# Attention of a two-block transformer on one core: the reciprocals' diagonal on ScalarE, the normed output kept in PSUM, and a new order of the projections

## The reference

```python
# first block: 8 local heads, each 64 wide, on an 8 x 64 grid
scores = jnp.einsum('brqhd,brkhd->bhrqk', qg, kn) * (dh ** -0.5) + bias[None]
p = jax.nn.softmax(jnp.where(mask, scores, NEG_INF), axis=-1)
o = jnp.einsum('bhrqk,brkhd->brqhd', p, vn)
# and 12 dilated heads in 3 groups (dilation 1, 4, 16), merged by their log-denominators
# second block: 16 query heads, 4 key heads, 512 latent and 256 context tokens
def gqa_attend(q, k, v):
    s = jnp.einsum('bkgqd,bksd->bkgqs', q, k, preferred_element_type=jnp.float32) * (HEAD_DIM_2 ** -0.5)
    p = jax.nn.softmax(s, axis=-1).astype(v.dtype)
    return jnp.einsum('bkgqs,bksd->bkgqd', p, v)
```

## Time and profile before

| | us |
|---|---|
| median of 3 runs | 2993.64 |
| lowest, highest | 2989.40, 2996.92 |
| the profiled execution | 3000.23 |
| its span, first to last instruction | 2998.4 |
| mean granted TensorE clock | 0.957 of full |

### The profile page before, as it was taken

How to read it: one execution, slowest core, us unless ns; L and a number is a source line. 1 busy time by engine, 2 the same in 40 slices (tenths; PEclk the granted TensorE clock), 3 DMA queues, 4 the chain that set the end, 5 groups by cost and what they waited for, 6 DMA issues and landing times. The chain is left out here.

```text
span 2998.4 us, 37915 instructions
## 1 busy us (share of the span) xinstructions
PE 2673.7 (89%) x14592; PEld 2178.1 (73%) x14592; DVE 1583.5 (53%) x2351; ACT 1041.3 (35%) x1815; POOL 1144.4 (38%) x654
## 2 busy tenths in 40 slices
PE   1799889989999888889699999997899999699998
PEld 1576567768887666666488888885787888488886
DVE  2444536654454436556665555555567686522223
ACT  2343333332222444444421122114456555422222
POOL 2235534534444422232333333333344444344443
PEclk9899999989999899999799999998899999799999
DMA  5444214433343100000133333321111111022221
GB/s 198 150 166 148 92 61 140 137 127 134 120 140 127 36 22 19 19 19 26 43 131 114 109 126 126 113 99 51 46 51 56 43 57 57 22 92 93 97 99 70
DMA packets 80547, 267.74 MB, mean 89 GB/s; under 512 B 8560, under 2 KB 14320, under 8 KB 80368
## 3 DMA queue, kind: packets, MB, share of 16 engines
q1 hardware_dynamic: 70416, 248.67, 24.0%
q10 hardware_dynamic: 9664, 15.34, 1.6%
q0 software_dynamic: 288, 1.31, 0.1%
HBM read 260.57 MB, written 4.72 MB: 88 GB/s over the span
## 5 line engine op out<-in xcount | busy, mean ns | idle before, releaser
L1975 POOL TENSOR_TENSOR SLO<-RAW,SHI 128x1024 fp32r<-128x1024 f32 (+1 forms) x336 | 817.0, 2433 | 1309.2 <-ACT SHI L1809 1309.0
L1809 ACT ACTIVATE SHI<-RAW 128x1024 fp32r<-128x1024 f32 (+1 forms) x336 | 346.3, 1033 | 1117.5 <-PE PS L2238 1084.6
L2236 PE MATMUL PS<-HLh,SHI 128*128 128x512 f32 x1680 | 690.3, 411 | 28.2 <-DVE HLl L2044 17.6
L2237 PE MATMUL PS<-HLl,SHI 128*128 128x512 f32 x1680 | 662.6, 394 | 0.0
L2238 PE MATMUL PS<-HLh,SLO 128*128 128x512 f32 x1680 | 662.2, 394 | 0.0
L2236 PEld LDWEIGHTS PS<-HLh,SHI 128*128 128x128 f32 x1680 | 320.2, 191 | 128.2 <-issue 48.3
L2238 PEld LDWEIGHTS PS<-HLh,SLO 128*128 128x128 f32 x1680 | 319.6, 190 | 69.2
L2236 PE MATMUL PS<-hh,SHI 128*128 128x512 f32 (+1 forms) x944 | 356.4, 378 | 13.3 <-DVE hl L2128 9.9
L2237 PEld LDWEIGHTS PS<-HLl,SHI 128*128 128x128 f32 x1680 | 320.8, 191 | 65.0 <-issue 7.0
L2237 PE MATMUL PS<-hl,SHI 128*128 128x512 f32 (+1 forms) x944 | 348.6, 369 | 0.0
L2238 PE MATMUL PS<-hh,SLO 128*128 128x512 f32 (+1 forms) x944 | 348.3, 369 | 0.0
(11 more groups left out here) (233 smaller groups left out, 4015.8 us busy)
## 6 DMA issues: line engine op xcount, KB each, us to landing
RAW<-in_k_w SPq DMA_DIRECT2D x316, 512.0 KB, 3.2
ADA<-in_k_w SPq DMA_DIRECT2D x132, 512.0 KB, 4.1
early<-in_k_w SPq DMA_DIRECT2D x12, 512.0 KB, 10.0
RAW<-in_k_w SPq DMA_DIRECT2D x20, 256.0 KB, 2.6
XL<-in_xT ACTq DMA_DIRECT2D x1, 2048.0 KB, 12.5
bi<-in_k_bias ACTq DMA_DIRECT2D x16, 128.0 KB, 3.0
out<-XL SPq DMA_DIRECT2D x8, 256.0 KB, 2.1
bi<-in_k_bias ACTq DMA_DIRECT2D x8, 192.0 KB, 3.7
```

The lines of the kernel that those rows point to most:

```text
L1809: eng.activation(u.hi, u.w, ACT.Copy).then_inc(S["a_hi"], 1)
L1975: eng.tensor_tensor(u.lo, u.w, u.hi.bitcast(F32), ALU.subtract).then_inc(S["g_lo"], 1)
L2236: eng.matmul(st.out, lh, rh, start=st.first and j == 0, stop=False)
L2237: eng.matmul(st.out, lh, rl, start=False, stop=False)
```

## The change

The reciprocals' diagonal is made by ACT, as a copy of the identity with the reciprocal as scale, in place of POOL. Its place in a round moves: first reciprocals and diagonals, then the output split. `onorm` writes its product to columns 256 to 383 of the bank itself, and the split reads it from there; the bank is given back after the low half. Empty yields ahead of a rotated projection's key are four and not two. The first local pair and its values go into the dense list, and the list has another order: v 0 comes right behind k 0, v 1 behind k 1, v 2 behind the second dilated group; the turned values (a write to memory and a read in another order) move with them.

```diff
@@ attention
-            t_rec, t = tick("v_rec"), tick("g_share")
+            t_rec, t = tick("v_rec"), tick("a_share")
...
-            put(OutNorm(b.ap, o.ap, t_mm, o.free, t_rb, t))
-            give(b, t)
-            return o, t
+            put(OutNorm(b.ap, o.ap, b.ap[:, 256:384], t_mm, o.free, t_rb, t))
+            o.free = [t]
+            return b, t
...
+            if turn:
+                for it in pairs[i - 2]:
+                    shares(it)
             if read:
                 finish(pairs[i - 3][0], *done)
                 if "done" in pairs[i - 3][1]:
                     emitted.add(pairs[i - 3][1]["done"])
-            if turn:
-                for it in pairs[i - 2]:
-                    shares(it)
...
-    def out_split(o, t_o, src, hi, lo, t_free):
+    def out_split(bank, t_o, src, hi, lo, t_free):
         t1, t2 = tick("a_ohi"), tick("v_olo")
         put(OutSplit(src, hi, lo, t_o, t_free, t1, t2))
-        o.free = [t1, t2]
+        give(bank, t2)
         return [t1, t2]
@@ dl_qk, and the same in qk2
-            yield
-            yield
+            for _ in range(4):
+                yield
             emitted.add(f"dilated {which} {g} {j}")
@@ the first attention
-    run(bgz(pipelined([na_qk(0, "q"), na_qk(0, "k")])))
...
-    for j in range(1, 4):
+    for j in range(4):
         dense += [after(f"na {j - 2} scored")] if j > 1 else []
         dense += [na_qk(j, "q")]
-        dense += [dl_turned(j - 2)] if j > 1 else []
-        dense += [na_qk(j, "k"), dl_values(j - 1)]
-    dense += [dl_qk(0, 0, "q"), dl_turned(2), dl_qk(0, 0, "k")]
-    dense += [dl_qk(0, g, w) for g in (1, 2) for w in "qk"]
+        dense += [dl_turned(j - 1)] if 0 < j < 3 else []
+        dense += [na_qk(j, "k")]
+        dense += [dl_values(j)] if j < 2 else []
+    dense += [dl_qk(0, g, w) for g in range(2) for w in "qk"]
+    dense += [dl_values(2), dl_qk(0, 2, "q"), dl_turned(2), dl_qk(0, 2, "k")]
@@ ScalarE
+            def share(st):
+                a.wait_ge(st.t_rec, st.t_dfree, d_const)
+                eng.activation(st.dg, ident, ACT.Copy, scale=st.m[:, 3:4]).then_inc(S["a_share"], 1)
@@ GpSimd
-            def share(st):
-                g.wait_ge(st.t_rec, st.t_dfree, d_const)
-                eng.tensor_scalar(st.dg, ident, st.m[:, 3:4], None, ALU.mult).then_inc(S["g_share"], 1)
@@ VectorE, onorm
-                eng.tensor_tensor(st.o, st.o, st.bank[:, 0:128], ALU.mult).then_inc(S["v_onorm"], 1)
+                eng.tensor_tensor(st.out, st.bank[:, 0:128], st.o, ALU.mult).then_inc(S["v_onorm"], 1)
```

More of the change, by code:

```diff
@@ L181 @@
 Pv = namedtuple("Pv", "p nk bank values dg t_p t_v t_dg t_bank t_mm")
-OutNorm = namedtuple("OutNorm", "bank o t_mm t_free t_rb t_done")
+OutNorm = namedtuple("OutNorm", "bank o out t_mm t_free t_rb t_done")
 OutSplit = namedtuple("OutSplit", "src hi lo t_in t_free t_hi t_lo")
@@ L1002, in na_items, with na_make @@
         return res
-    def na_make(it, o, t_o):
+    def na_make(it, b, t_o):
         j, t = it["j"], it["t"]
         v = lambda a: a.rearrange("p (r c) -> p c r", r=8)[:, 16 * t:16 * t + 16, :]
-        src = o.ap.rearrange("p (c r) -> p c r", r=8)
-        oa_rdy[j] += out_split(o, t_o, src, v(oa[j][0]), v(oa[j][1]), [])
+        src = b.ap[:, 256:384].rearrange("p (c r) -> p c r", r=8)
+        oa_rdy[j] += out_split(b, t_o, src, v(oa[j][0]), v(oa[j][1]), [])
     vb = W["vb"].cells[0].ap.rearrange("p (g t n) -> p g t n", g=3, t=4)
@@ L1087, in dl_items, with dl_make @@
         return res
-    def dl_make(it, o, t_o):
+    def dl_make(it, b, t_o):
         j, r = it["j"], it["r"]
-        ob_rdy[j] += out_split(o, t_o, o.ap, ob[j][0][:, r:NT:4], ob[j][1][:, r:NT:4],
+        ob_rdy[j] += out_split(b, t_o, b.ap[:, 256:384], ob[j][0][:, r:NT:4], ob[j][1][:, r:NT:4],
                                [mtok(0, 47)] if j else [])
@@ L1140, in build_program @@
     dense += [some(bg, 32)]
-    first_out = lambda it, o, t: (na_make if "t" in it else dl_make)(it, o, t)
+    first_out = lambda it, b, t: (na_make if "t" in it else dl_make)(it, b, t)
     weave((attention(heads, W, first_out), 0.6), (bgz(pipelined(dense)), 1.0))
@@ L1358, in att_items, with make2 @@
         return res
-    def make2(it, o, t_o):
+    def make2(it, b, t_o):
         h, c0 = it["hs"], it["c0"]
@@ L1363, in make2 @@
             h.rdy = []
-        h.rdy += out_split(o, t_o, o.ap, h.hi[:, c0:c0 + 128], h.lo[:, c0:c0 + 128], h.free)
+        h.rdy += out_split(b, t_o, b.ap[:, 256:384], h.hi[:, c0:c0 + 128], h.lo[:, c0:c0 + 128], h.free)
     def out2(i, hs, stats=()):
@@ L1954, in _ @@
             own = {Dma: dma_, Table: table, Silu: silu_c, Split: split, Square: square_, Rstd: rstd_, NormA: norm_a,
-                   VCopy: vcopy, HSq: hsq, HNorm: hnorm, Score: score, Flip: flip_, OutNorm: onorm, OutSplit: osplit, Gate: gate,
+                   VCopy: vcopy, HSq: hsq, HNorm: hnorm, Score: score, Flip: flip_, Share: share, OutNorm: onorm, OutSplit: osplit, Gate: gate,
                    GSum: gsum, SiluF: silu, Up: up, LowerB: lowerb, Sigm: sigm, GateF: gate_f, GateX: gate_x,
@@ L2013, in lev_a @@
                     eng.tensor_tensor(r, r, st.q, ALU.mult).then_inc(S["g_lev"], 1)
-            own = {Dma: dma_, Split: split, Square: square_, HRope: hrope, Share: share, GateX: gate_x, DiagK: diag_k,
+            own = {Dma: dma_, Split: split, Square: square_, HRope: hrope, GateX: gate_x, DiagK: diag_k,
                    ScanQ: scan_q, LevA: lev_a}
```

## The result

The changed kernel takes 3004.47 us (median of 6 runs, 3002.88 to 3009.57) against 2992.90 for the kernel before in the same runs: ratio 1.0041, 95% interval 1.0028 to 1.0054. It is 11.6 us slower, where 12 us faster was forecast. The profiled execution has a span of 3001.9 us.

What follows compares the result with a forecast made beforehand. PE was taken as busiest but not full, with about 80 us idle in the attention stretches. First attention -17.5 and second +5.8 make about -12 us: 2981.6 against the median 2993.64; forecast alone 2973 to 2990, whole range 2966 to 3004.

Steps and rivals of the forecast that it cites:

- The diagonal's earlier time: PE's waits for dg shorten: first attention -13.4 us in local heads, -3.6 and +1.8 in dilated rounds; second -2.6 and -4.0.
- four waits in the dilated rounds: First attention: half of these waits for dg go, 2.6 us, plus 1.0 us of slow matmuls, together -3.6.
- What ScalarE adds: Second attention: diagonals at 0.40 us each make maxima up to 0.8 us later; +6 us, bounds 0 and +26.
- Output kept in PSUM: Second attention: low half no longer stretched, -2.6 us; held bank makes flips wait, +9 us, bounds 0 and +20.
- Later release: Empty yields are flushed with the tail, so waits for rotated q and k stay: 0, within 2 us.
- Rival 3: Later release does delay scores and covers part of four waits for rotated q: 9 us more, 2972; chance 0.13.
- First pair: First attention: waits at q 0 and k 0 covered, -5.7 us; flushed tails at k 2 +2.9, at d q 2 +0.5.
- The sum: First attention -17.5 us, second +5.8, net -11.7, say -12.
- rival 1: Loop through ScalarE and DVE decides, second attention +26 instead of +6: 3002 to 3009 us; chance 0.19 together with Rival 4.
- Rival 4: dg doesn't come earlier because ScalarE is late with splits: 3005 us; chance 0.19 together with rival 1.

Runs made afterwards that it cites:

- e9: Changed kernel with reciprocals and diagonals emitted behind the output split again; new order, held bank and four yields stay: ratio 0.9958 to the kernel before.
- e11: Kernel before with the diagonal on ScalarE in its old place behind the output split, output still through SBUF: ratio 0.9975.
- e7: Kernel before with the diagonal on ScalarE behind the output split, output in PSUM with the bank held, old order: 2974.89 us, ratio 0.9943.
- e4: Kernel before, unchanged, timed and profiled a second time: ratio 1.0001, span 2989.9 us.
- e5: Kernel before with the diagonal on ScalarE ahead of the output split and output in PSUM, old order, two yields: 3001.64 us, ratio 1.0030.
- e2: Kernel before with only the diagonal on ScalarE ahead of the output split; output in SBUF, old order: ratio 1.0021.
- e3: Kernel before with only the output kept in PSUM and the bank held; diagonal on GpSimd behind the split, old order: ratio 0.9998.
- e6: Changed kernel with two empty yields ahead of the keys in place of four: ratio 1.0041 to the kernel before.
- e8: Kernel before with waits for keys and turned values made part of neighbouring jobs, so they flush no tail: ratio 0.9994.
- e12: e7 with the first local pair joined to the head of the common sequence, rest of the old order kept: 2968.01 us, ratio 0.9916.
- e1: Kernel before with only the new order of projections; diagonal on GpSimd behind the split, output in SBUF: ratio 1.0067.
- e10: e5 with only VectorE's reciprocals ahead of the output split and ScalarE's diagonals behind the high half: 2968.76 us, ratio 0.9926.

## Why the prediction was wrong

The step that failed is the price of the diagonals' place ahead of the output split on ScalarE: +6 us, all of it in the second attention. With the diagonals put back behind the split and nothing else changed (e9), 24 us come back, from both attentions. The 18 us between price and cost are most of the 23.6 by which the forecast missed (-12 forecast, +11.6 measured). The other terms missed in both directions and left 6 us.

**The diagonal's earlier time.** Right in its mechanism: in the local heads the longest wait for dg is 0.65 us in the changed kernel, and was 3.1. The size was not: e11, which has the diagonal on ACT and nothing else, gains 5.9 us in the first attention, where the terms made 15.2 (13.4 and 3.6, less 1.8). With the low half unstretched too (e7) it is 11.9. 6.0 of the 13.4 were slow matmuls that I tied to the waits of the earlier trace rows; e4 has the same waits and slow matmuls behind one of the three. The profile that I read took 6.6 us more than the median, and I subtracted from the median what, in good part, only the slower execution had. Besides, half of the four waits in the dilated rounds, 7.8 us, is 3.9 and not the 2.6 that I wrote.

**What ScalarE adds.** The price of one was right, 0.40 us against

```profile
L1855 ACT ACTIVATE dg<-CONST,m x144: 384/391/406, 130.4 to 1458.0; 128x128 f32<-128x128 f32 x144
```

and so was the chain, high half behind both diagonals. The price, +6, was not. I let DVE's idle time absorb most of it because DVE was about half busy, and counted it in the second attention only. Measured by e5 against e7 the place costs 15.2 us there and 9.4 in the first. With the output in SBUF (e2 against e11) it is 3.6 and 7.4: so the 6 us would have done for the second attention without the held bank, and the first attention was left out in any case. DVE's idle time lies elsewhere in the round; in the round shown DVE waited 0.86 us where the chain runs, all of the 0.8 that I had allowed as the most. I had also seen place and engine as one step. They are two: on ACT behind the split the engine's change gives its gain without the chain. The Trainium skill (PSUM — Partial Sum Buffer, Engine vs sequencer instructions) says that ScalarE's queue is strictly first in, first out; the 1.55 us at 1122.04 agree.

**Output kept in PSUM.** That the low half is never stretched held (294 ns at most in the second attention of the changed kernel, 406 in the first), as did the port rule of the Trainium skill (SBUF — State Buffer, Who interferes with whom), by which this was to be expected: where the source stays in SBUF, as in e2, the maxima are 1491 and 2023 ns. DVE's write took 300 ns in PSUM for 288 in SBUF. The net, +9 less 2.6, was wrong alone: e3 shows -2.6 in the second attention. But the bank isn't free beside the diagonals' place: e5 less e2 is +8.8 there. The sum adds two terms, bank and place, each of which depends on the other.

**Later release.** Nothing, as predicted: e6 equals the change, and the waits for rotated q of the earlier trace rows are there at 4.5 and 4.9 us. Rival 3, which gave 9 us to covering them, falls with it, and e8 shows that taking the flushes away gives nothing in the kernel before.

**First pair.** -5.7, +2.9 and +0.5 were to make -2.3. The first is about right: both waits of the earlier trace rows are gone in the changed kernel and in e12, and joining the pair alone gains 3.0 us by the profiles and 8 by the ratios. So is the second: behind k 2 the changed kernel waits 1.69 us for the square at 191.17 and 1.20 for qa at 194.85. What failed is that I priced the order only at its own ends. The new order costs 21 us alone (e1) and, beside the diagonal on ACT in its old place, 7.3 in the first attention (e9 less e7; by the ratios 0.15%, with intervals that overlap). In e1 the local heads meet rotations on POOL ahead of their diagonals. In the changed kernel, where POOL makes no diagonals, the local heads have four waits of 0.87 us for the norm's logarithm at 209 to 247 us, which e7 and e12 haven't. How the rest is made up stays open.

**The sum.** Second attention +5.8 forecast, +10.9 measured, past the 3 to 9 that the prediction allowed. First attention -17.5 forecast, +5.3 measured against e4. The runs make up both stages: in the first, -11.9 with everything in its good place (e7 less e4), +9.9 for the place (changed less e9) and +7.3 for the order (e9 less e7) are the +5.3; in the second, -6.7, +17.2 and +0.4 are the +10.9. The result lies in the range of rival 1, 3002 to 3009 by the loop through ScalarE and DVE, and the loop is what e5, e7 and e10 show. But its number is luck: its terms make about +26 in the second attention and -17.5 in the first, and the measured +10.9 and +5.3 only happen to give a sum as large. Rival 4 falls, since dg was early.

## What to carry to other kernels

When work moves to another engine, its place in that engine's queue is a separate choice: put it behind what others wait for, and ahead of it only if its own input is sure to be there. That an engine is idle half of the time doesn't mean that it absorbs a wait in a loop that passes through it each round. Before a term of a few us is read from one profile, take a second profile of the same kernel. Try the parts of a change alone and in pairs: here the move gained 0.6% in one place with the bank and lost 0.3% in the other.

## What was not expected of the hardware

Two profiles of the same kernel differ by 6.3 us in the first attention and not at all in the second, with granted clocks of 0.93 and 0.96 over 181 us of the local heads. Three waits of PE are the same to 0.01 us in both, and slow matmuls follow all three in one execution and one of them in the other. The high half of the split is quicker from PSUM on ACT, a median of 254 ns in the changed kernel's second attention against 302 before, which I hadn't counted. The low half's median there is 291 ns for 284, and the copy of the shares stayed at 277.
